# Chunk stage of an RWKV-7 layer: level products on four quarters of TensorE, X by transposes, one projection laid in eight pieces between them

## What is computed

```python
def wkv7_step(state, inp):
    r, w, k, v, a, b = inp
    sa = jnp.einsum('...ij,...j->...i', state, a)
    state = (state * w[..., None, :] + sa[..., :, None] * b[..., None, :]
             + v[..., :, None] * k[..., None, :])
    y = jnp.einsum('...ij,...j->...i', state, r)
    return state, y
# per direction: q = p + mu * (shifted - p); r, k, v, wd, ad = split(q)
# kk = k * k_k / |k * k_k|;  a = -kk, b = kk * sigmoid(...);  y of both directions is summed,
# normed per head, and r*k*r_k summed per head times v is added
```

## Time and profile before

| | us |
|---|---|
| three runs, median | 4460.75 (4459.96 to 4464.31) |
| the profiled execution, device time | 4463.06 |
| span of its trace | 4461.3 |
| the 16 steps of the stage, in the trace | 3577.0 to 4353.0 |
| granted TensorE clock, mean over the span | 0.983 |

### The profile page before, as it was taken

How to read it: one execution, slowest core, us unless ns; L and a number is a source line. 1 busy time by engine, 2 the same in 40 slices (tenths; PEclk the granted TensorE clock), 3 DMA queues, 4 the chain that set the end, 5 groups by cost and what they waited for, 6 DMA issues and landing times. The chain is left out here.

```text
span 4461.3 us, 75646 instructions
## 1 busy us (share of the span) xinstructions
PE 4257.6 (95%) x31548; PEld 3234.5 (73%) x31548; DVE 2500.3 (56%) x4058; ACT 1603.2 (36%) x2471; POOL 328.6 (7%) x313
## 2 busy tenths in 40 slices
PE   8898999999999999999999999989999999999988
PEld 6675788786788777888888644467888567776775
DVE  4635534434545352777776579965544255666663
ACT  2315322323322232666666410043222233334432
POOL 0030000000000000111111000000000022221220
PEclk9898999999999999999999999999999999999999
DMA  4202222221122322111121322222222210000101
GB/s 155 114 21 76 91 98 95 89 95 76 67 103 95 137 109 92 55 55 57 49 62 50 132 76 76 76 76 76 95 104 101 105 40 21 21 22 21 37 25 57
DMA packets 37634, 334.90 MB, mean 75 GB/s; under 512 B 4192, under 2 KB 6496, under 8 KB 19680
## 3 DMA queue, kind: packets, MB, share of 16 engines
q1 hardware_dynamic: 37344, 330.66, 20.2%
HBM read 318.06 MB, written 12.58 MB: 74 GB/s over the span
## 5 line engine op out<-in xcount | busy, mean ns | idle before, releaser
L654 PE MATMUL ps<-hi,weight_parts 128*128 128x512 f32 x3072 | 956.7, 391 | 26.7 <-DVE lo L430 17.9
L642 DVE TENSOR_TENSOR weight_parts<-w,weight_parts 128x1024 fp32r<-128x1024 f32 (+1 forms) x327 | 398.0, 1218 | 906.6 <-ACT weight_parts L633 906.1
L633 ACT ACTIVATE weight_parts<-w 128x1024 fp32r<-128x1024 f32 (+1 forms) x327 | 344.0, 1053 | 999.7 <-PE ps L654 906.5
L654 PEld LDWEIGHTS ps<-hi,weight_parts 128*128 128x128 f32 x3072 | 579.7, 189 | 156.2 <-issue 23.5
L654 PE MATMUL ps<-lo,weight_parts 128*128 128x512 f32 x1536 | 599.9, 391 | 0.0
L4272 PEld LDWEIGHTS ps<-buffers 64*64 64x64 f32 x12544 | 412.4, 135 | 127.0 <-issue 126.7
L654 PE MATMUL ps<-hidden_high,weight_parts 128*128 128x512 f32 x1536 | 491.4, 399 | 12.6 <-DVE hidden_low L428 12.6
L4272 PE MATMUL ps<-buffers 64*64 64x64 f32 x12544 | 438.8, 224 | 42.2 <-issue 18.9
L2817 PE MATMUL ps<-x_parts,column_parts 128*128 128x512 f32 x1536 | 360.3, 392 | 4.9 <-DVE column_parts L3068 4.4
L654 PEld LDWEIGHTS ps<-hidden_high,weight_parts 128*128 128x128 f32 x1536 | 290.5, 189 | 79.7 <-issue 17.4
L654 PEld LDWEIGHTS ps<-lo,weight_parts 128*128 128x128 f32 x1536 | 290.0, 189 | 60.3 <-issue 0.2
(11 more groups left out here) (584 smaller groups left out, 5849.9 us busy)
## 6 DMA issues: line engine op xcount, KB each, us to landing
w<-in_weights SPq DMA_DIRECT2D x121, 2048.0 KB, 8.0
w<-in_wh SPq DMA_DIRECT2D x64, 512.0 KB, 4.0
buffers<-in_weights SPq DMA_DIRECT2D x3, 2048.0 KB, 12.3
x_kept<-x SPq DMA_DIRECT2D x2, 2048.0 KB, 6.9
v_kept<-buffers SPq DMA_DIRECT2D x4, 1024.0 KB, 5.2
buffers<-v_kept SPq DMA_DIRECT2D x16, 256.0 KB, 2.6
x<-in_xT SPq DMA_DIRECT2D x4, 512.0 KB, 11.3
h<-in_pw SPq DMA_DIRECT2D x2, 1024.0 KB, 5.9
```

Source lines behind the costliest of these rows:

```text
L633: act.activation(K.parts[:, j % 2, 0, 0:nk, :], part_of(K, slot, j, nk, by_row), ACT.Copy)\
L642: dve.tensor_tensor(K.parts[:, j % 2, 1, 0:nk, :], part_of(K, slot, j, nk, by_row), K.parts[:, j % 2, 0, 0:nk, :].bitcast(F32), ALU.subtra ...
L654: mm = pe.matmul(ps, K.parts[:, j % 2, m, k, :], x[:, k * T:(k + 1) * T], start=(first and k == 0 and n == 0), stop=(last and k == nk - 1 ...
```

## The change

- **Quarters.** The 16 matmuls of `t` and of `ct` are no longer all on the two diagonal quarters of the array. For a pair u of blocks (e = 0, 1) and head h, `t` takes rows of h and writes partitions of e, `ct` takes rows of e and writes partitions of h; so T1 lies by block parity on partitions and by (u, head) in the free dimension. The four quarters stand one behind the other, and each row half writes its own bank. Halves "a" and "b" are gone: one ACT copy of 128x512 and one DVE add of 128x512 for a level.
- **X by transposes.** `cx`, its DVE adds, `x0` and POOL's identity for X are gone. At the start of each of the five levels PE transposes XT in four 128x128 pieces into bank 2, and DVE copies them to X. The first waits for `mrk`, since the score products lie in banks 2 and 3; each further one waits for the add of the level before.
- **The second projection** (2d+1, bank 3) is no longer in the front between `ch_g(1)` and `ch_sa(1)`. Each of its eight matmuls is a `piece`: in levels 1 to 3 one ahead of `ct` and one ahead of `ch_ys`, in levels 4 and 5 one ahead of `ch_ys`. ACT's copy of it (`keep`, for d = 1 with Silu) goes from the front to the end of the step.

```diff
@@ POOL
-                pool.tensor_copy(X, on_chunks("cident")).then_inc(GM.step("ix"), 1)
                 pool.tensor_copy(XT, on_chunks("cident")).then_inc(GM.step("ixt"), 1)
@@ PE
+            quarters = ((0, 0), (1, 1), (0, 1), (1, 0))
...
+                def piece(k):
+                    if nth is None:
+                        return
+                    if k == 0:
+                        pe.wait_ge(K.sem("raw_kept"), K.count("raw_kept", 4 * (c + 1) + 2 * d))
...
+                    mm = pe.matmul(K.ps[:, 3, :], w[:, k, m * P:(m + 1) * P], K.H[:, k, :], start=(k == 0), stop=(k == 7),
+                                   skip_group_check=True)
...
                 ch_g(p, pd, 1)
-                if n is not None:
-                    projection(1)
                 ch_sa(p, pd, 1)
...
                 for l in levels:
                     if n is not None:
-                        pe.wait_ge(GM.sem, GM.count(n, f"c{l}"))
-                        for half in "ab":
-                            pe.wait_ge(DM.sem, DM.count(n, f"xt{l - 1}{half}" if l > 1 else "x0"))
-                            for j in chunks_of(half):
-                                mm = heads(block_of(0, j), C[:, j, :], XT[:, j, :])
...
-                    if n is not None and l < 5:
-                        for half in "ab":
-                            for j in chunks_of(half):
-                                mm = heads(block_of(2, j), T1[:, j, :], X[:, j, :])
...
+                        for u in range(4):
+                            mm = pe.transpose(K.ps[:, 2, u * P:(u + 1) * P],
+                                              XT[:, 2 * u:2 * u + 2, :].rearrange("p e t -> p (e t)"), K.c("ident"))
+                        mm.then_inc(PM.step(f"xr{l - 1}"), 1)
+                        pe.wait_ge(GM.sem, GM.count(n, f"c{l}"))
+                        for u in range(4):
+                            for h, e in quarters:
+                                mm = pe.matmul(two_banks(0)[hr(e), u, h, :], paired(C)[hr(h), u, e, :],
+                                               paired(XT)[hr(h), u, e, :], start=True, stop=True, skip_group_check=True)
+                        mm.then_inc(PM.step(f"t{l}"), 1)
+                    ch_g(p, pd, l + 2)
+                    if n is not None and l < 4:
+                        piece(2 * (l - 1))
...
+                    ch_sa(p, pd, l + 2)
+                    if n is not None:
+                        piece(2 * l - 1 if l < 4 else l + 2)
                     ch_ys(p, pd, l + 2)
@@ ACT
-                        for half in "ab":
-                            act.activation(in_half(T1, half), bank_half(0, half), ACT.Copy)\
-                               .then_inc(AM.step(f"t{l}{half}"), 1)
+                        act.activation(paired(T1), two_banks(0), ACT.Copy).then_inc(AM.step(f"t{l}"), 1)
@@ DVE, levels
+                        dve.wait_ge(PM.sem, PM.count(n, f"xr{l - 1}"))
+                        dve.tensor_copy(X.rearrange("p j t -> p (j t)"), K.ps[:, 2, :]).then_inc(DM.step(f"x{l - 1}"), 1)
                     gk(p, pd, l + 2)
...
+                        dve.tensor_tensor(paired(XT if l < 5 else XTC[:, d]), paired(XT), two_banks(4), ALU.add)\
+                           .then_inc(DM.step(f"xt{l}"), 1)
                     upd(p, pd, l + 2)
```

More of the change, by code:

```diff
@@ L4430, in step @@
-                    ch_sa(p, pd, l + 2)
-                    if n is not None and l < 5:
                         if l == 1:
                             pe.wait_ge(DM.sem, DM.count(n, "mrk"))
-                            K.apart(pe)
-                        for half in "ab":
-                            for j in chunks_of(half):
-                                mm = heads(block_of(2, j), T1[:, j, :], X[:, j, :])
-                            mm.then_inc(PM.step(f"cx{l}{half}"), 1)
+                        else:
+                            pe.wait_ge(DM.sem, DM.count(n, f"xt{l - 1}"))
@@ new lines, in step @@
+                        mm.then_inc(PM.step(f"t{l}"), 1)
[3 more added lines that the diff above has]
+                    if n is not None:
+                        pe.wait_ge(AM.sem, AM.count(n, f"t{l}"))
+                        pe.wait_ge(DM.sem, DM.count(n, f"x{l - 1}"))
+                        K.apart(pe)
+                        for u in range(4):
+                            for e, h in quarters:
+                                mm = pe.matmul(two_banks(4)[hr(h), u, e, :], paired(X)[hr(e), u, h, :],
+                                               paired(T1)[hr(e), u, h, :], start=True, stop=True, skip_group_check=True)
+                        mm.then_inc(PM.step(f"ct{l}"), 1)
@@ L4530, in step @@
                                           .rearrange("p n o -> p (n o)"), ACT.Copy).then_inc(AM.step("ee"), 1)
-                    if nth is not None:
-                        if d == 1:
-                            act.wait_ge(K.sem("fin_dve"), K.count("fin_dve", 4 * c))
-                        keep(c + 1, 1 - par, 2 * d + 1)
                 san(p, pd, 1)
@@ L4544, in step @@
                     if n is not None:
-                        for half in "ab":
-                            act.wait_ge(PM.sem, PM.count(n, f"t{l}{half}"))
-                            act.activation(in_half(T1, half), bank_half(0, half), ACT.Copy)\
-                               .then_inc(AM.step(f"t{l}{half}"), 1)
+                        act.wait_ge(PM.sem, PM.count(n, f"t{l}"))
+                        act.activation(paired(T1), two_banks(0), ACT.Copy).then_inc(AM.step(f"t{l}"), 1)
                     san(p, pd, l + 2)
+                if nth is not None:
+                    if d == 1:
+                        act.wait_ge(K.sem("fin_dve"), K.count("fin_dve", 4 * c))
+                    keep(c + 1, 1 - par, 2 * d + 1)
             for m in range(4):
```

67 lines of the change are left out of this document (23 added, 44 removed).

## The result

The changed kernel takes 4500.73 us (median of four runs, 4497.04 to 4502.87); the kernel before, on the same chip, 4461.97 (4459.96 to 4464.31). The ratio is 1.0082, with a 95% interval of 1.0070 to 1.0095. The kernel is slower by 0.8%, inside the range and 8 us above the forecast of 4493.

The account below looks back on a forecast made before the run. Levels bound by PE's rate of 64-column passes, the front by PE (d = 0) or nearly DVE (d = 1). 12 x (4.6 - 2.05) = +31, +32 with the other steps: 4495, median 4493 us; range 4455 to 4560.

Parts of the forecast that it names:

- The levels: Five levels per step, each the sum of PE's work: 5.05 us for levels 1 to 3, 4.33 for 4 and 5.
- the stretch: From the end of mrk to the next step's wa: 23.9 us forecast against 19.28 before, 4.6 more per step.
- a burst: 32 passes of t or ct, ten times per step: four quarters at a time, 14.6 ns a pass, 0.47 us.
- (1): Rival: quarters don't run four at a time or PE can't take in passes so fast; up to 4568 us, chance 0.23.
- (2): Rival: the way in and out of whole-array operations is hidden, a piece costs 0.86 us; 4433 us, chance 0.13.
- The "issue" breaks: PE breaks of 0.18 and 1.21 us in step 4's levels before; forecast gone, since fewer and longer instructions are asked for.
- yields nothing: Per step, removing cx saves 3.74 us of PE and five sets of transposes cost 3.85.
- Levels without pieces: Steps 14 and 15: 3.59 us a level, 18.1 for five against 20.4 and 19.9 before, -4 us together.
- The front: Part of a step before the levels, without the second projection: 3.7 us won for d = 0, 0.4 for d = 1.
- the walk through the queues: Operation-by-operation timing of the front without the second projection: 3.9 us won for d = 0, 0.65 for d = 1.
- rival (4): PE idling before tb lowers the clock in d = 1 fronts: up to 3 us in six steps, +18, 4511; no separate chance.

Follow-up runs that it names:

- block: Changed kernel with the second projection put back as one block in front, quarters and transposes kept: 4464.8 us, ratio 1.0003 to the kernel before.
- late: As block, but in each level the quarter products with C precede the transposes, whose copies DVE and ACT share: 4486.15 us, ratio 1.0048.
- busy: Changed kernel with unread products added in front ahead of tb, one for d = 0, five for d = 1: 4481.31 us, ratio 1.0045.
- mixed: As busy, but d = 1 steps have the second projection as a block in front and no filling products: 4465.96 us, ratio 1.0004.
- pairs: Changed kernel with the sixteen quarter products of a level product reordered, the eight of the diagonal quarters first: 4518.58 us.
- few: As block, with eight unread quarter products of 256 columns added in each level ahead of ct: 4529.31 us.
- many: As block, with 32 unread quarter products of 64 columns added in each level ahead of ct: 4597.91 us.
- pieces_only: Kernel before with only the second projection laid in eight pieces between the levels, and cx moved to one bank: 4539.94 us.

## Why the prediction was right

**The levels.** The sum stood as written: 5.05 us for levels 1 to 3 (5.00 measured), 4.33 for 4 and 5 (4.37), 23.9 for the stretch (23.62). So did its terms: a piece 1.06 (1.05), a burst first to last start 0.47 (0.48 in the pass records of L4432 in step 4, 0.51 to the next line). Rivals (1) and (2) are out: quarters run four at a time, and each piece pays for the switch. The "issue" breaks left the levels that hold pieces, as forecast; the reason given, that fewer and longer instructions are asked for, had no price. That the exchange of `cx` for transposes "yields nothing" holds for PE's time: a set of transposes holds 0.59 us and the twelve passes ahead of it take 0.49 for 0.35, 0.73 in all, five sets 3.65 against 3.74 for `cx`. Block can't test it, since it changes the quarters too. Where no pieces stand, the transposes are also a part of the chain: late, which takes them off it (and halves DVE's copy and moves `SE`), has 3.29 and 3.42 us a level against 3.79.

**Levels without pieces** were put at 3.59 us, 18.1 for five; block and step 14 have 18.83 and 18.88. That sum of PE's work and two waits was short of the chain by 0.2 us a level. It is a part of why steps 14 and 15 did not give their 4 us. The rest is in step 15: without pieces the break is back. In level 2 of the changed kernel PE stops for 0.89 us at "issue" inside L4444, half clock follows, and levels 2 and 3 take 4.93 and 4.84 us where the others take 3.8.

**The front** is the term that was mis-sized: 2.05 us a step forecast, 17.06 / 12 = 1.42 measured, 7.5 us over the twelve steps. At full clock the walk through the queues was right (busy: 4.0 and 0.7 where 3.9 and 0.65 were walked; with the longer d = 1 fronts of before, 31.58 on average, it is 367.74 - 337.33 = 30.4 in twelve). What took 13.35 of these 30.4 is rival (4), the lower clock. The prediction looked for it only in the d = 1 fronts, up to 3 us each, and put it on top of the sum instead of into it; it came in all twelve fronts, for 3.4 us in d = 0 and 6.8 in d = 1.

**The sum.** +34.0 us measured on the span, +32 forecast. That it is so near is in part luck, since the misses cancel: front +7.5, steps 14 and 15 +4, levels -3, step 1 -1, the stage's earlier start -5. The 8 us between 4493 and 4500.73 come from there only by 2; the rest is how each profiled execution lies to the median: before it was 1 to 2 us above, after (4497.04) it is the lowest of four. Why the stage begins earlier in the kernels with pieces in d = 0 steps (3571.7 to 3574.2) than in those without (3576.2 to 3577.0) was not looked into.

**What the forecast lacked** is a limit that it hardly needed: the supply of instructions. The earlier trace rows showed it, as 1.21 and 0.18 us at "issue". In the steps with pieces it fell away by itself, since a piece holds PE for 1.05 us with four records. It decides, however, whether any way of making these levels denser is worth something, and none of the versions here beats the kernel before: block and mixed are even with it.

**Open.** Not known is what makes the same 1.49 us wait cost the clock in every d = 0 front of the kernel after and in none of pairs. Why step 0 of block falls to the lower clock for its whole length of levels was not tried by itself; few, with more products in the same levels, has it for 3.4 us only, and takes 23.3 us from `mrk` to `wa` against block's 23.48, so there the added products cost nothing. Quarter products in two halves, which would shorten the chain, were not tried either, nor a way to ask for fewer instructions.

## What to carry to other kernels

Work moved into idle time of another part costs only what it adds to the chain there, but count what it leaves behind: a front that now waits can lose the clock, and the slowed products behind the wait come back as time. When a change makes bursts of small products shorter, look next at who waits for the burst (copies and additions in series) and at how many instructions per microsecond the stretch asks for. Breaks put down to "issue" in the middle of a burst of one line, which end soon after an instruction transfer has landed (1.2 to 1.6 us here), are that limit.

## What was not expected of the hardware

- Each quarter of the array starts a pass of 64 columns some 58 ns after its last, and quarters start 6 to 7 ns apart: 14.6 ns a pass on average. PE passes over waiting products to start later ones on a free quarter, within limits (pairs).
- Instructions of PE come in blocks of 16384 bytes, no closer than 3.3 us in any of these kernels. Levels of some 200 records in 3.5 us (late) or 328 in 4.7 (many) run dry, for 0.6 to 2.5 us at a time.
- A 1.5 us wait of PE in a d = 0 front is followed by 3.4 us at half clock in all six fronts of the kernel after, in four of six of pieces_only, and in none of six of pairs, where nothing fills it. With one product of 128x128x512 in it the clock is whole in six of six (busy).
- DVE's `SE`, a product of 128x64, takes 0.25 us in one place and 1.02 in the other. In the kernel after it starts at 3799.65 and ends at 3800.67, while POOL's C runs from 3799.35 to 3800.62. In late, where it stands ahead of C, it takes 0.25:

```profile
3799.35 1.27 POOL L4251 TENSOR_TENSOR buffers<-buffers,const 128x512 f32<-128x512 f32 x1 [4.47 <-PE ps L4432]
...
3799.65 1.02 DVE L4573 TENSOR_SCALAR buffers<-buffers 128x64 f32<-128x64 f32 x1
```

```profile
3963.87 0.25 DVE L4586 TENSOR_SCALAR buffers<-buffers 128x64 f32<-128x64 f32 x1
...
3964.36 1.27 POOL L4251 TENSOR_TENSOR buffers<-buffers,const 128x512 f32<-128x512 f32 x1 [2.98 <-PE ps L4429]
```

The Trainium skill, "SBUF — State Buffer", section "SBUF: two separate sides", has a lock on a pair of ports that VectorE and GpSimd share, held for a whole instruction; it concerns VectorE's instructions in a mode that uses both of its ports or with two inputs in SBUF. The trace agrees as far as it can show this: 1.02 us, up to 0.05 us behind the end of POOL's instruction. In the stage of the kernel after, all 56 that start beside one of POOL's products end 0.05 us behind it, and the 45 others take 0.24 to 0.29. Which mode `SE` runs in no trace shows.
